# A one-core inference step: first expert rows prepared for two experts at a time, 22 leading weight slots instead of 20, residual rows behind the second expert, gathers of 96 rows

## The chip, the cores and the metric

The kernel runs on one core of a Trainium2 chip. TensorE does the matmuls, VectorE and ScalarE move and scale results, GpSimd issues the gathers, and SyncE issues the weight transfers; 16 DMA engines carry them out. The metric is the device time of one execution in microseconds, as the median of several runs.

## The reference

One layer of a hybrid encoder over 256 prompt tokens and 32 sample tokens, all in fp32. An attention and a recurrent branch are mixed and added to x; then a mixture of experts follows, the part that matters here:

```python
def hmoe(h, wg, bg, ws, bs, wu, wd):
    ...
    _, g_idx = lax.top_k(g_logits, 1)
    ...
    e_val, e_idx = lax.top_k(sub_sel, TOP_K)
    ...
    for e in range(N_EXPERTS):
        gate, up = jnp.split(hf @ wu[e], 2, axis=-1)
        out = out + combine[:, e:e + 1] * ((jax.nn.silu(gate) * up) @ wd[e])
```

There are 16 experts in 4 groups of 4. A token picks one group and two experts in it. An expert has 2048 x 1024 up-weights (8 MB) and 512 x 2048 down-weights (4 MB), so 192 MB of expert weights are read.

## The kernel before

The program is one stream of instructions for each engine, joined by semaphores. Up to about 1187 us it computes the projections, the two branches and W_O, with a ring of four weight tiles. Then a router stage picks groups and experts, and after it the expert stage reads all 16 experts.

**Pieces and slots.** Expert weights come in 192 pieces of 1 MB, in the order of `STREAM`: eight up-pieces of expert 0, then a mix in which two up-pieces of the next expert and one down-piece of this one alternate. Piece n goes to slot `SLOT[n]`. There are 16 permanent slots (`PERM`) and 4 that are used once (`ONCE`), because they lie in memory that later holds something else: two under `yo` and `gain`, two under the second half of `hgs`. SyncE's loop has a wait ahead of some pieces: n = 14 for the end of W_O, n = 17 for the x1 rows to be written out, the first gather and its tail (`x1_out`, `token_ps`, `xs_in`). From n = 20 a piece waits until TensorE has used the piece that was last in its slot (`eh_done`). For n = 20 to 32 that is piece n - 20, from n = 33 on piece n - 16. Down-pieces of the last expert are cut by halves.

**Rows of a group.** For a group of experts (`g`), GpSimd gathers the up to 96 token rows of that group from x1 in memory into `xs` (`rows_in`, L688). `spread` (L1421) multiplies them with one-hot matrices `R`, so that `hgs` holds the rows, transposed, in 64 slots of each of four experts: 16 blocks k of 128 channels. ScalarE and VectorE drain each step with the norm's gain `gup` (`drain_spread`). For group 0 there are four such steps q, with two spreads to each engine: q = 0 and 1 before the first piece, q = 2 and 3 ahead of half-pieces t = 2 and t = 4 (`SPREAD_AT`). For the next groups they lie among the down-pieces of the third expert of the group before.

**Half-pieces.** The expert loop counts t from 0 to 383, two for each piece. `column_pair` (L1396) does the four matmuls of a half. `row_turn` (L1411, L1415) turns the one-hot matrices at t = 8 (`FIRST_ROWS`); `act_turn` (L1453) turns an expert's activation before its down-pieces, which begin at `DOWN_AT` (20, 44, 68, ... for experts 0, 1, 2). `meta_turn` (L1405) makes the next group's metadata at `META_AT`, the next rows are turned at `ROWS_AT`, and `residual` (L1446) adds the gathered rows to the four output banks at `RESIDUAL_AT`, which also frees `xs` for the next gather. In the kernel before all of these stand in the down-phase of a group's first expert. `add_rows` (L1462) adds an expert's result to the output banks. `keep_warm` issues matmuls whose result nobody reads.

Of the kernel before, what the change touches and what calls it, by code (L numbers as in the profile page):

```python
# [14 lines left out]
F32 = mybir.dt.float32  # L15
# [7 lines left out]
P = 128  # L23
# [27 lines left out]
PERM, ONCE = 16, 4  # L51
# [23 lines left out]
SLOT = [*range(13), *range(PERM, LEAD), *range(13, PERM)] + [n % PERM for n in range(PIECES - LEAD)]  # L75
# [43 lines left out]
NCONST, NCONST2 = 21, 13  # L119

# [33 lines left out]
def build(nc, x_prompt, x_sample, cache_k, cache_v, state_conv, state_lru, norm1_g, w_in, conv_w,  # L154
# [128 lines left out]
    lgT = sb("lgT", [40, T])  # L283
    best = sb("best", [TB, 5, 5 * FT, 4])
# [7 lines left out]
    hgs = sb("hgs", [P, 2, KT, EPG, ES])  # L292
    at_hgs1 = here[0] - 2 * 8192
# [33 lines left out]
    xs = sb("xs", [P, D])  # L327
    at_yo = here[0]
    yo = sb("yo", [CAP, D])
    gain = sb("gain", [P, D])  # L330
# [30 lines left out]
    up_v = expert_w_up[0].rearrange("e (p k) n -> p e k n", k=KT)  # L361
# [11 lines left out]
    with ExitStack() as ctx:  # L373
# [10 lines left out]
        trio = [bank[0:2], bank[2:4], bank[4:6]]  # L384

        x_in = [sem(f"x_in{f}") for f in range(FT)]
        par_in, rw_in, gain_in, gup_in = sem("par_in"), sem("rw_in"), sem("gain_in"), sem("gup_in")
# [58 lines left out]
        def spread_bank(q, c):  # L446

            return trio[q % 3][c] if q < SPREAD else work
# [15 lines left out]
        def _(sp):  # L464
# [12 lines left out]
            sp.dma_start(gup[:, :], norm2_g[0].rearrange("(p k) -> p k", k=KT)).then_inc(gup_in, 16)  # L477
# [53 lines left out]
            for dst, src in ((wr[:, :, 0:4], router_group_w[0].rearrange("(k p) g -> p k g", p=P)),  # L531
# [4 lines left out]
                sp.dma_start(dst, src).then_inc(rw_in, 16)  # L536
            gated_loads(T_PA, COL["ga"], w_pa_v)

            def fetch(slot, e, s, by_half=False):

                dst = raw[slot][:, :]
                if s < PU:
                    src = up_v[:, e, 2 * s:2 * s + 2, :]
                    dst = dst.rearrange("p (a k n) -> p a k n", a=1, k=2)
# [19 lines left out]
            for n, (e, s) in enumerate(STREAM):  # L564
# [41 lines left out]
        def _(pool):  # L606
# [122 lines left out]
        def _(a):  # L729
# [247 lines left out]

            def drain_spread(q):

                a.wait_ge(spreadA_ps, q + 1)  # L980
                for c in range(2):
                    k = 4 * (q % SPREAD) + c
                    ins = a.activation(hgs[:, q // SPREAD % 2, k, :, :].rearrange("p e s -> p (e s)"),
                                       spread_bank(q, 0)[:, 256 * c:256 * (c + 1)], ACT.Copy, scale=gup[:, k:k + 1])
# [58 lines left out]
            a.wait_ge(gup_in, 16)  # L1043
            for q in range(2):
                drain_spread(q)
            for t in range(HALF_N):
# [16 lines left out]
                if t == FIRST_ROWS:  # L1063
                    rows(0, bank[2])
# [3 lines left out]
                for q, at in enumerate(SPREAD_AT):  # L1068
                    if t == at[0]:
# [14 lines left out]
            with a.If(n > CAP):  # L1084
                def again(v, first, width):

                    with a.Fori(0, NG) as g:
                        with a.Fori(0, width) as w:
# [5 lines left out]
                            for k in range(KT):  # L1094
                                a.wait_ge(ovhg_ps, KT * it + k + 1)
                                a.activation(hgs[:, 0, k, :, :].rearrange("p e s -> p (e s)"),
                                             bank[4 + k % 4][:, 0:EPG * ES], ACT.Copy, scale=gup[:, k:k + 1])\
# [29 lines left out]
        def _(pe):  # L1127
            pe.wait_ge(consts2, NCONST2)
            pe.wait_ge(par_in, 16 * 9)
# [1005 lines left out]
```

## Time and profile before

| what | value |
|---|---|
| median of 3 runs | 1687.1 us (1686.56 to 1687.59) |
| profiled execution, its time | 1686.14 us |
| profiled execution, its span | 1684.3 us |
| TensorE busy | 1610.3 us, 96% |
| VectorE, ScalarE, GpSimd busy | 720.2, 639.7, 139.1 us |
| DMA, SyncE's queue | 383.31 MB in 391456 packets |

Busy time of TensorE is modelled and holds matmuls that wait in a pipeline, so its 96% alone doesn't say that it bounds the kernel. The time of the profiled execution is 1.8 us more than its span, and 1.0 us less than the median.

### The profile page before, as it was taken

The page shows a single profiled execution, that of the slowest core. Times are in us where ns is not written, and L with a number is a line of the kernel's source. Part 1 is how long each engine was busy: PE and PEld are TensorE (multiplying, and loading weights), DVE is VectorE, ACT ScalarE, POOL GpSimd, SP SyncE. Part 2 cuts the span into 40 slices and gives each one's busy share as a digit, 9 for nine tenths or more (in the row PEclk, how much of TensorE's full clock was granted, in tenths as well). Part 3 has the DMA queues.
Part 4 walks back from the last instruction along what each step waited for, and adds up shares of the span by engine and source line. Part 5 has one row for each costly group of instructions (what it writes and reads, how often), then busy time and mean ns, then how long its engine had stood idle before and what let it go on. Part 6 is the DMA issues. An engine that isn't in the chain of part 4 may idle for free. (4 is left out here: it accounts for less than half of the span.)

```text
span 1684.3 us, 27482 instructions
## 1 busy us (share of the span) xinstructions
PE 1610.3 (96%) x10714; PEld 1295.7 (77%) x10714; DVE 720.2 (43%) x1072; ACT 639.7 (38%) x1078; POOL 139.1 (8%) x189
## 2 busy tenths in 40 slices
PE   5999999999999999999999999999999999989885
PEld 4999999999999999999999999999734334323221
DVE  5888886443445455455454444544310201101101
ACT  6666665333344444444443333544211211111202
POOL 1644441000000000000000000000000000000000
PEclk9999999999999999999999999999999999999998
DMA  8465556566656546546478567795899999999995
GB/s 215 129 165 159 152 160 177 150 172 177 189 145 190 146 139 189 151 133 187 86 202 217 150 168 188 207 298 180 301 359 422 421 421 421 421 421 421 422 421 233
DMA packets 404519, 400.28 MB, mean 238 GB/s; under 512 B 19504, under 2 KB 377248, under 8 KB 379392
## 3 DMA queue, kind: packets, MB, share of 16 engines
q1 hardware_dynamic: 391456, 383.31, 69.2%
q0 software_dynamic: 2560, 11.21, 2.1%
q10 hardware_dynamic: 10432, 4.79, 1.1%
q8 instruction: 47, 0.77, 0.2%
q14 instruction: 24, 0.20, 0.0%
HBM read 389.77 MB, written 13.43 MB: 239 GB/s over the span
## 5 line engine op out<-in xcount | busy, mean ns | idle before, releaser
L1164 PE MATMUL bank<-hH,wH 128*128 128x288 f32 x1792 | 536.1, 299 | 6.2 <-ACTq L799 2.7
L1615 DVE TENSOR_TENSOR wL<-ring,wH 128x1024 fp32r<-128x1024 f32 x320 | 387.9, 1230 | 353.7 <-ACT wH L736 346.1
L736 ACT ACTIVATE wH<-ring 128x1024 fp32r<-128x1024 f32 x320 | 335.6, 1058 | 517.3 <-PE bank L1166 446.8
L1165 PE MATMUL bank<-hL,wH 128*128 128x288 f32 x1792 | 528.9, 295 | 0.0
L1166 PE MATMUL bank<-hH,wL 128*128 128x288 f32 x1792 | 528.5, 295 | 0.0
L1164 PEld LDWEIGHTS bank<-hH,wH 128*128 128x128 f32 x1792 | 337.3, 188 | 13.5 <-issue 7.0
L1165 PEld LDWEIGHTS bank<-hL,wH 128*128 128x128 f32 x1792 | 337.4, 188 | 0.3
L1166 PEld LDWEIGHTS bank<-hH,wL 128*128 128x128 f32 x1792 | 337.2, 188 | 0.0
L1396 PE MATMUL bank<-raw,hgs 128*64 128x512 f32 x1024 | 242.7, 600 | 18.9 <-DMA raw<-in_expert_w_up 15.3
L1396 PEld LDWEIGHTS bank<-raw,hgs 128*64 128x64 f32 x1024 | 66.6, 136 | 162.2 <-issue 110.5
L1164 PE MATMUL bank<-oH,wH 128*128 128x288 f32 x512 | 150.7, 294 | 0.5 <-DVE oL L1712 0.5
L1165 PE MATMUL bank<-oL,wH 128*128 128x288 f32 x512 | 151.0, 295 | 0.0
L1166 PE MATMUL bank<-oH,wL 128*128 128x288 f32 x512 | 150.9, 295 | 0.0
L1396 PE MATMUL bank<-raw,actT 128*64 128x512 f32 x512 | 124.7, 601 | 8.3 <-DMA raw<-in_expert_w_down 7.8
L1984 DVE SCALAR_TENSOR_TENSOR silu<-bank,es,silu 64x512 f32<-64x512 f32 x16 | 12.1, 757 | 265.7 <-ACT silu L1020 265.7
L1164 PEld LDWEIGHTS bank<-oH,wH 128*128 128x128 f32 x512 | 96.3, 188 | 1.0 <-DVE oL L1712 0.7
L1165 PEld LDWEIGHTS bank<-oL,wH 128*128 128x128 f32 x512 | 96.3, 188 | 0.0
L1166 PEld LDWEIGHTS bank<-oH,wL 128*128 128x128 f32 x512 | 96.2, 188 | 0.0
L1396 PEld LDWEIGHTS bank<-raw,actT 128*64 128x64 f32 x512 | 32.9, 136 | 78.3 <-issue 56.8
L1020 ACT ACTIVATE silu<-bank,es 64x512 f32<-64x512 f32 x16 | 10.9, 681 | 198.7 <-PE bank L1396 198.6
L1350 PE MATMUL bank<-hH,wH 128*128 128x288 f32 x256 | 76.4, 299 | 0.0
L1351 PE MATMUL bank<-hL,wH 128*128 128x288 f32 x256 | 75.5, 295 | 0.0
(312 smaller groups left out, 1538.4 us busy)
## 6 DMA issues: line engine op xcount, KB each, us to landing
raw<-in_expert_w_up SPq DMA_DIRECT2D x128, 1024.0 KB, 26.0
ring<-in_w_in SPq DMA_DIRECT2D x112, 1024.0 KB, 6.3
raw<-in_expert_w_down SPq DMA_DIRECT2D x64, 1024.0 KB, 26.5
ring<-in_w_pb SPq DMA_DIRECT2D x16, 1024.0 KB, 9.1
ring<-in_w_pa SPq DMA_DIRECT2D x16, 1024.0 KB, 9.1
ring<-in_w_o SPq DMA_DIRECT2D x16, 1024.0 KB, 6.1
cK<-in_cache_k SPq DMA_DIRECT2D x16, 256.0 KB, 2.8
cV<-in_cache_v SPq DMA_DIRECT2D x16, 256.0 KB, 3.2
```

The costliest lines, as they stand in the source:

```text
L736: a.activation(wH[2 * (slot % 2) + half][:, :, :], ring[slot][:, 8 * half:8 * half + 8, :], ACT.Copy).then_inc(hi_ready, 1)
L1020: a.activation(silu[ES:P, :], upb[0:ES, :], ACT.Silu, scale=es[0:ES, e // EPG % 2, e % EPG, 4:5]).then_inc(silu_ready, 1)
L1164: pe.matmul(dst, hi, rH[:, k, :], start=(k == 0), stop=False)
L1165: pe.matmul(dst, hi, rL[:, k, :], start=False, stop=False)
L1166: ins = pe.matmul(dst, lo, rH[:, k, :], start=False, stop=(k == KT - 1))
L1350: pe.matmul(dst, hi, hH[:, k, :], start=(k == 0), stop=False, skip_group_check=True)
L1351: pe.matmul(dst, hi, hL[:, k, :], start=False, stop=False, skip_group_check=True)
L1396: ins = pe.matmul(dst[c * ES:(c + 1) * ES, :], w, raw[slot][:, 1024 * half + 512 * c:1024 * half + 512 * (c + 1)], start=first, stop=last)
L1615: v.tensor_tensor(lo[:, :, :], ring[slot][:, 8 * half:8 * half + 8, :], hi[:, :, :].bitcast(F32), ALU.subtract).then_inc(lo_ready, 1)
L1984: v.scalar_tensor_tensor(silu[ES:P, :], upb[ES:P, :], es[ES:P, e // EPG % 2, e % EPG, e % EPG:e % EPG + 1], silu[ES:P, :], ALU.mult, ALU.m ...
```

## The change

- **Slots.** Six single-use slots instead of four, 22 leading pieces instead of 20. They lie under `yo` and `gain` (two), under the part of `hgs` for experts 2 and 3 of group 0 (one), under the second half of `hgs` (two), and under the scratch of W_O's end, where `yH` and `yL` will be (one). `hgs` is laid out by pairs of experts. SyncE's wait for the end of W_O moves from n = 14 to n = 13, the wait for x1 and the gather from n = 17 to n = 18. The first piece that waits for n - 16 is now n = 35.
- **First rows by pairs.** For group 0 a spread makes 128 columns, for two experts. The first pair has two steps of eight spreads: q = 0 before the first piece, q = 1 at t = 4 and t = 8. The second pair follows at t = 31, 33, 35 and 37. `FIRST_ROWS` moves from t = 8 to t = 12 and to another bank.
- **Channel order.** Block k now holds channels of the two-by-two order `(s p k)`: `spread` reads `xs` with a step of 2 elements instead of 16, up-pieces are one run of 1 MB in memory, and `gup` is read as 1024 runs of 8 bytes instead of 128 of 64, on the semaphore that TensorE's first instruction waits for.
- **Next group's work and residual** move from the down-phase of a group's first expert to that of its second; `add_rows` of the first expert now starts the sum, and the residual is added to it.
- **96 rows** in the gathers and in `gain`, not 128. A memset of unused indices is gone. `keep_warm(14)` instead of `keep_warm(6)` ahead of the metadata.

```diff
-PERM, ONCE = 16, 4
+PERM, ONCE = 16, 6
...
-SLOT = [*range(13), *range(PERM, LEAD), *range(13, PERM)] + [n % PERM for n in range(PIECES - LEAD)]
+SLOT = [*range(13), PERM + 2, PERM, PERM + 1, *range(PERM + 3, LEAD), *range(13, PERM)] + [n % PERM for n in range(PIECES - LEAD)]
...
-ASSIGN_AT = [DOWN_AT[EPG * g] for g in range(NG - 1)]
-META_AT = [DOWN_AT[EPG * g] + 2 for g in range(NG - 1)]
-ROWS_AT = [DOWN_AT[EPG * g] + 6 for g in range(NG - 1)]
-RESIDUAL_AT = [DOWN_AT[EPG * g] + 10 for g in range(NG)]
-FIRST_ROWS = 8
-SPREAD_AT = [(None, None)] * 2 + [(2, 2), (4, 4)]
+ASSIGN_AT = [DOWN_AT[EPG * g + 1] for g in range(NG - 1)]
+META_AT = [DOWN_AT[EPG * g + 1] + 2 for g in range(NG - 1)]
+ROWS_AT = [DOWN_AT[EPG * g + 1] + 6 for g in range(NG - 1)]
+RESIDUAL_AT = [DOWN_AT[EPG * g + 1] + 4 for g in range(NG)]
+FIRST_ROWS = 12
+SPREAD_AT = [(None, None), (4, 8)] + [(DOWN_AT[0] + 11 + 4 * r, DOWN_AT[0] + 13 + 4 * r) for r in range(2)]
...
-    hgs = sb("hgs", [P, 2, KT, EPG, ES])
-    at_hgs1 = here[0] - 2 * 8192
+    at_hgs = here[0]
+    hgs = sb("hgs", [P, 2, 2, KT, 2, ES])
...
-    xs = sb("xs", [P, D])
+    xs = sb("xs", [CAP, D])
...
-    here[0] = at_hgs1
-    raw += [sb(f"raw{s}", [P, 2048]) for s in range(PERM + 2, LEAD)]
+    here[0] = at_hgs + 8192
+    raw += [sb(f"raw{s}", [P, 2048]) for s in range(PERM + 2, PERM + 5)]
     assert here[0] <= at_o
+    here[0] = at_prow
+    raw += [sb(f"raw{s}", [P, 2048]) for s in range(PERM + 5, LEAD)]
...
-    up_v = expert_w_up[0].rearrange("e (p k) n -> p e k n", k=KT)
+    up_v = expert_w_up[0].rearrange("e (s p k) n -> p e s k n", p=P, k=2)
...
-            return trio[q % 3][c] if q < SPREAD else work
+            return out4[2 * q + c] if q < 2 else work
...
-            sp.dma_start(gup[:, :], norm2_g[0].rearrange("(p k) -> p k", k=KT)).then_inc(gup_in, 16)
+            sp.dma_start(gup[:, :].rearrange("p (s k) -> p s k", k=2),
+                         norm2_g[0].rearrange("(s p k) -> p s k", p=P, k=2)).then_inc(par_in, 16)
...
-                elif n == 14:
+                elif n == 13:
                     sp.wait_ge(half_done, 2 * T_END)
-                elif n == 17:
+                elif n == 18:
+                    sp.wait_ge(lg_ps, 1)
                     sp.wait_ge(x1_out, 16 * len(X1_PARTS) + 16)
                     sp.wait_ge(token_ps, 2)
                     sp.wait_ge(xs_in, 16)
...
-                    sp.dma_start(gain[:, :], final_norm_g.rearrange("(a n) -> a n", a=1).partition_broadcast(P))\
+                    sp.dma_start(gain[:, :], final_norm_g.rearrange("(a n) -> a n", a=1).partition_broadcast(CAP))\
...
-                                            bass.IndirectOffsetOnAxis(ap=idx[:, column, 2:3], axis=0),
+                                            bass.IndirectOffsetOnAxis(ap=idx[0:CAP, column, 2:3], axis=0),
...
-                    pool.wait_ge(outB, SPREAD * (g + 1))
...
+            def drain_pair(q):
+
+                a.wait_ge(spreadA_ps, q + 1)
+                for c in range(4):
+                    k = 8 * (q % 2) + 4 + c
+                    ins = a.activation(hgs[:, 0, q // 2, k, :, :].rearrange("p e s -> p (e s)"),
+                                       spread_bank(q, 1)[:, P * c:P * (c + 1)], ACT.Copy, scale=gup[:, k:k + 1])
+                ins.then_inc(outA, 1)
...
-            a.wait_ge(gup_in, 16)
-            for q in range(2):
-                drain_spread(q)
+            a.wait_ge(par_in, 16 * NPARAM)
+            drain_pair(0)
...
-            def spread(dst, k):
-
-                return pe.matmul(dst.rearrange("p (e s) -> p e s", e=EPG), xs[0:CAP, k::KT], R[:, :, 0, :].bitcast(F32),
+            def spread(dst, k, first=0, count=EPG):
+
+                c = 2 * P * (k // 2) + k % 2
+                return pe.matmul(dst.rearrange("p (e s) -> p e s", e=count), xs[:, c:c + 2 * P - 1:2],
+                                 R[:, first:first + count, 0, :].bitcast(F32),
                                  start=True, stop=True, skip_group_check=True)
 
+            def pair_step(q, c):
+
+                if q >= 2 and c == 0:
+                    need(pe, outA, q if q > 2 else 0)
+                elif q >= 2:
+                    pe.wait_ge(outB, q + 1)
+                if q == 0 and c == 0:
+                    pe.wait_ge(xs_in, 16)
+                    pe.wait_ge(R_ready, 1)
+                if q == 1 and c == 1:
+                    pe.wait_ge(last_ready, 1)
+                dst = spread_bank(q, c)
+                for kk in range(4):
+                    ins = spread(dst[:, P * kk:P * (kk + 1)], 8 * (q % 2) + 4 * c + kk, 2 * (q // 2), 2)
+                ins.then_inc((spreadB_ps, spreadA_ps)[c], 1)
...
-            keep_warm(6)
+            keep_warm(14)
             pe.wait_ge(meta_ready, 1)
             meta_turn(0, bank[6])
             keep_warm(20)
-            for q in range(2):
-                spread_step(q, 0)
-                spread_step(q, 1)
+            pair_step(0, 0)
+            pair_step(0, 1)
...
-                    if j == 0 and g > 0:
+                    if j == 0 and g > 0 or e == 2:
                         pe.wait_ge(outA, SPREAD * (g + 1))
...
                 if e == 0 and s < PU and half == 0:
-                    pe.wait_ge((outA, outB)[s % 2], s // 2 + 1)
+                    pe.wait_ge((outB, outA)[s // 2 % 2], s // 4 + 1)
...
-                    add_rows((e - 1) // EPG % 2, (e - 1) % EPG, j == 0)
+                    if j == 1:
+                        pe.wait_ge(es_ready, g + 1)
+                        pe.wait_ge(RT_ready, g + 1)
+                        need(pe, scaled_ready, 4 * g)
+                    add_rows((e - 1) // EPG % 2, (e - 1) % EPG, j == 0, j == 1)
...
                 for g_ in range(NG):
                     if t == RESIDUAL_AT[g_]:
-                        pe.wait_ge(es_ready, g_ + 1)
-                        pe.wait_ge(RT_ready, g_ + 1)
-                        need(pe, scaled_ready, 4 * g_)
-                        residual().then_inc(xs_free, 1)
+                        residual(False).then_inc(xs_free, 1)
...
-            own.step(v.memset(idx[CAP:P, :, 2:3], 0))
...
+            def drain_pair(q):
+
+                v.wait_ge(spreadB_ps, q + 1)
+                k = 8 * (q % 2)
+                v.tensor_tensor(hgs[:, 0, q // 2, k:k + 4, :, :].rearrange("p k e s -> p k (e s)"),
+                                spread_bank(q, 0)[:, :].rearrange("p (k c) -> p k c", k=4),
+                                gup[:, k:k + 4].rearrange("p (k a) -> p k a", a=1).to_broadcast([P, 4, 2 * ES]),
+                                ALU.mult).then_inc(outB, 1)
```

TensorE at the start of the expert stage, before the change. R and xs are the spreads, raw the weight pieces by buffer number, ms and ident the row turn:

```order
L1320 MATMUL bank<-hH 128x288 x20
L1421 MATMUL bank<-R,xs 128x256 x8
L1396 MATMUL bank<-raw_136,hgs 64x512 x4
L1421 MATMUL bank<-R,xs 128x256 x4
L1396 MATMUL bank<-raw_137,hgs 64x512 x4
L1421 MATMUL bank<-R,xs 128x256 x4
L1396 MATMUL bank<-raw_138,hgs 64x512 x4
L1396 MATMUL bank<-raw_139,hgs 64x512 x4
L1411 MATMUL bank<-ident,R 128x96 x4
L1415 MATMUL bank<-ms,R 128x5 x4
```

The same place after it:

```order
L1336 MATMUL bank<-hH 128x288 x20
L1438 MATMUL bank<-R,xs 128x128 x8
L1412 MATMUL bank<-raw_136,hgs 64x512 x4
L1412 MATMUL bank<-raw_137,hgs 64x512 x4
L1438 MATMUL bank<-R,xs 128x128 x4
L1412 MATMUL bank<-raw_138,hgs 64x512 x4
L1412 MATMUL bank<-raw_139,hgs 64x512 x4
L1438 MATMUL bank<-R,xs 128x128 x4
L1412 MATMUL bank<-raw_140,hgs 64x512 x4
L1412 MATMUL bank<-raw_141,hgs 64x512 x4
L1427 MATMUL bank<-ident,R 128x96 x4
L1431 MATMUL bank<-ms,R 128x5 x4
```

There are as many spreads ahead of the row turn, 16, each of half the columns, and they stand further apart.

TensorE in the down-phase of expert 0, before the change, from its first down-piece (raw_181) to the last piece that stands ahead of the limit (the one behind raw_190):

```order
L1396 MATMUL bank<-raw_181,actT 64x512 x4
L1405 MATMUL bank<-meta,G 96x12 x3
L1396 MATMUL bank<-raw_182,hgs 64x512 x4
L1396 MATMUL bank<-raw_183,hgs 64x512 x4
L1411 MATMUL bank<-ident,R 128x96 x4
L1415 MATMUL bank<-ms,R 128x5 x4
L1396 MATMUL bank<-raw_187,actT 64x512 x4
L1396 MATMUL bank<-raw_188,hgs 64x512 x4
L1446 MATMUL bank<-xs,ident 96x512 x4
L1396 MATMUL bank<-raw_189,hgs 64x512 x4
L1396 MATMUL bank<-raw_190,actT 64x512 x4
L1396 MATMUL bank<-raw_160,hgs 64x512 x4
```

The same down-phase after it, from the sixth piece on, with the rows around the second pair:

```order
L1412 MATMUL bank<-raw_188,hgs 64x512 x2
L1438 MATMUL bank<-R,xs 128x128 x4
L1412 MATMUL bank<-raw_188,hgs 64x512 x2
L1412 MATMUL bank<-raw_190,actT 64x512 x2
L1438 MATMUL bank<-R,xs 128x128 x4
L1412 MATMUL bank<-raw_190,actT 64x512 x2
L1412 MATMUL bank<-raw_191,hgs 64x512 x2
L1438 MATMUL bank<-R,xs 128x128 x4
L1412 MATMUL bank<-raw_191,hgs 64x512 x2
L1412 MATMUL bank<-raw_192,hgs 64x512 x2
L1438 MATMUL bank<-R,xs 128x128 x4
L1412 MATMUL bank<-raw_192,hgs 64x512 x2
```

The metadata turn, the row turn and the residual have left this phase, and four steps of four spreads have come into it.

## Rows read from the trace of the kernel before

**Rows 1.** Page, the span in 40 slices: DMA busy, in tenths.
```profile
DMA  8465556566656546546478567795899999999995
```

**Rows 2.** Waits, 1600 to 1665 us: total, times, longest.
```profile
PE bank L1396 <- DMA raw<-in_expert_w_up: 6.1, 11, 0.6
```

**Rows 3.** Stretches: length, busy of each engine (instructions), granted clock, DMA share, GB/s.
```profile
1200.00:1205.00 5.00, 5.00 (x27) 5.00 (x27) 1.52 (x9) 0.00 (x0) 0.00 (x0) 0.66 0.59 209
1225.00:1230.00 5.00, 3.37 (x18) 1.01 (x16) 1.02 (x3) 0.68 (x1) 0.00 (x0) 1.00 1.00 390
1245.00:1250.00 5.00, 5.00 (x16) 1.61 (x16) 0.00 (x0) 0.00 (x0) 0.74 (x1) 1.00 0.64 262
1250.00:1255.00 5.00, 5.00 (x26) 1.72 (x24) 0.00 (x0) 0.00 (x0) 1.35 (x2) 1.00 0.74 228
1300.00:1340.00 40.00, 40.00 (x186) 14.49 (x184) 5.66 (x8) 5.79 (x12) 0.00 (x0) 1.00 1.01 421
```

**Rows 4.** Timeline of SyncE: start us, us, then line, operation and count.
```profile
1180.52 0.43 SPq L552 DMA_DIRECT2D raw<-in_expert_w_down  x1
1187.76 1.07 SPq L552 DMA_DIRECT2D raw<-in_expert_w_up  x2
1188.88 0.66 SPq L552 DMA_DIRECT2D raw<-in_expert_w_down  x1
...
1239.91 14.12 SPq L552 DMA_DIRECT2D raw<-in_expert_w_up  x2
```

**Rows 5.** Timeline of TensorE, matmul records: start, us, operation, count, [idle before].
```profile
1199.73 0.68 PE L1405 MATMUL bank<-meta,G 96*96 96x12 f32 x6 [1.32 <-DVEq L1948]
1200.26 4.43 PE L1320 MATMUL bank<-hH 128*128 128x288 f32 x20
1204.53 3.81 PE L1421 MATMUL bank<-R,xs 96*128 96x256 f32 x16
1208.27 1.94 PE L1396 MATMUL bank<-raw,hgs 128*64 128x512 f32 x8
1210.14 2.15 PE L1421 MATMUL bank<-R,xs 96*128 96x256 f32 x8
...
1219.74 0.55 PE L1411 MATMUL bank<-ident,R 96*128 96x96 f32 x4
...
1221.04 7.09 PE L1396 MATMUL bank<-raw,hgs 128*64 128x512 f32 x32
1229.76 1.94 PE L1396 MATMUL bank<-raw,hgs 128*64 128x512 f32 x8 [1.63 <-DVE silu L1984]
...
1235.60 0.68 PE L1405 MATMUL bank<-meta,G 96*96 96x12 f32 x6
...
1244.68 3.67 PE L1446 MATMUL bank<-xs,ident 96*96 96x512 f32 x8
```

**Rows 6.** Timeline of GpSimd, 1190 to 1255 us.
```profile
1198.02 1.12 POOL L688 DMA_INDIRECT xs<-x_rows,idx  x1 [10.32 <-DVE idx L1925]
```

**Rows 7.** DMA issues, us to landing: 1187 to 1200, then 1265 to 1600.
```profile
xs<-x_rows,idx POOLq DMA_INDIRECT x1, 6.1
...
xs<-x_rows,idx POOLq DMA_INDIRECT x2, 9.8
```

**Rows 8.** Groups, 1190 to 1260 us: busy us, mean ns, idle before.
```profile
L1421 PEld LDWEIGHTS bank<-R,xs 96*128 96x128 f32 x32 | 7.3, 307 | 1.6 <-issue 1.6
...
L1975 DVE TENSOR_TENSOR hgs<-bank,gup 128x512 f32<-128x512 f32 x4 | 2.8, 691 | 12.1 <-PE bank L1421 12.1
...
L1415 PEld LDWEIGHTS bank<-ms,R 96*128 96x128 f32 x16 | 1.9, 192 | 0.0
```

**Rows 9.** DMA packets, 16 to 20 us, then 838 to 840 us.
```profile
DMA packets 2365, 1.20 MB, mean 301 GB/s; under 512 B 16, under 2 KB 2365, under 8 KB 2365
...
DMA packets 3625, 0.06 MB, mean 29 GB/s; under 512 B 3625, under 2 KB 3625, under 8 KB 3625
```

**Rows 10.** Timeline of ScalarE, 0 to 30 us.
```profile
19.16 2.00 ACT L736 ACTIVATE wH<-ring 128x1024 fp32r<-128x1024 f32 x2 [1.90 <-DMA ring<-in_w_in]
```

More of the change, by code:

```diff
@@ L283, in build @@
     lgT = sb("lgT", [40, T])
+    here[0] = max(here[0], at_prow + 8192)
     best = sb("best", [TB, 5, 5 * FT, 4])
@@ L982, in drain_spread @@
                     k = 4 * (q % SPREAD) + c
-                    ins = a.activation(hgs[:, q // SPREAD % 2, k, :, :].rearrange("p e s -> p (e s)"),
-                                       spread_bank(q, 0)[:, 256 * c:256 * (c + 1)], ACT.Copy, scale=gup[:, k:k + 1])
+                    ins = a.activation(hgs[:, q // SPREAD % 2, :, k, :, :].rearrange("p a e s -> p a (e s)"),
+                                       work[:, 256 * c:256 * (c + 1)].rearrange("p (a c) -> p a c", a=2),
+                                       ACT.Copy, scale=gup[:, k:k + 1])
                 ins.then_inc(outA, 1)
@@ L1063, in _ @@
                 if t == FIRST_ROWS:
-                    rows(0, bank[2])
+                    rows(0, bank[4])
                 for g in range(NG - 1):
@@ L1068, in _ @@
                 for q, at in enumerate(SPREAD_AT):
-                    if t == at[0]:
+                    if q < SPREAD and t == at[1]:
+                        drain_pair(q)
+                    elif q >= SPREAD and t == at[0]:
                         drain_spread(q)
@@ L1432, in spread_step @@
                     pe.wait_ge(outA, q + 1)
-                if q == 0 and c == 0:
-                    pe.wait_ge(last_ready, 1)
                 if r == 0 and c == 0:
@@ L1437, in spread_step, with residual @@
                     pe.wait_ge(R_ready, n + 1)
-                dst = spread_bank(q, c)
                 for kk in range(2):
-                    ins = spread(dst[:, 256 * kk:256 * (kk + 1)], 4 * r + 2 * c + kk)
+                    ins = spread(work[:, 256 * kk:256 * (kk + 1)], 4 * r + 2 * c + kk)
                 ins.then_inc((spreadA_ps, spreadB_ps)[c], 1)
-            def residual():
+            def residual(first):
                 for nb in range(4):
-                    ins = pe.matmul(out4[nb][0:CAP, :], ident[0:CAP, 0:CAP], xs[0:CAP, nb * 512:(nb + 1) * 512],
-                                    start=True, stop=False, skip_group_check=True)
+                    ins = pe.matmul(out4[nb][0:CAP, :], ident[0:CAP, 0:CAP], xs[:, nb * 512:(nb + 1) * 512],
+                                    start=first, stop=False, skip_group_check=True)
                 return ins
@@ L1454, in act_turn, with add_rows @@
                 ins.then_inc(at_ps, 1)
-            def add_rows(buf, j, last):
+            def add_rows(buf, j, last, first=False):
                 for half in range(2):
@@ L1462, in add_rows @@
                             ins = pe.matmul(out4[2 * half + c][0:CAP, :], RT[rows, buf, j, :], y[rows, half, :],
-                                            start=False, stop=last and y is yL, skip_group_check=True)
+                                            start=first and y is yH, stop=last and y is yL, skip_group_check=True)
                     ins.then_inc(sum_ps, 1)
@@ L1495, in _ @@
                     if t == TURN_AT[x]:
-                        if x % EPG == 1 and x // EPG + 1 < NG:
+                        if x % EPG == 2 and x // EPG + 1 < NG:
                             pe.wait_ge(RT_ready, x // EPG + 2)
@@ L1565, in again @@
                         pe.wait_ge(xs_in, 32 * (NG + nth) + 16)
-                        residual()
+                        residual(True)
                         with pe.Fori(0, width) as w:
@@ L2023, in _ @@
             v.tensor_copy(cnt_i[:, :], cmax[:, :]).then_inc(routed, 1)
-            v.wait_ge(gup_in, 16)
-            for q in range(2):
-                drain_spread(q)
+            v.wait_ge(par_in, 16 * NPARAM)
+            drain_pair(0)
             for t in range(HALF_N):
@@ L2041, in _ @@
                 if t == FIRST_ROWS:
-                    columns(bank[2], 0, 0)
+                    columns(bank[4], 0, 0)
                 for g in range(NG - 1):
@@ L2052, in _ @@
                 for q, at in enumerate(SPREAD_AT):
-                    if t == at[1]:
+                    if q < SPREAD and t == at[0]:
+                        drain_pair(q)
+                    elif q >= SPREAD and t == at[1]:
                         drain_spread(q)
```

49 lines of the change are left out of this document (27 added, 22 removed).

## The prediction

> **What bounds the kernel now.** I read the page's forty slices first [rows 1]: the DMA engines are busy 4 to 8 tenths in the first 26 slices, and 9 tenths or more in every slice from 30 to 39. The last third, the expert stage, is held by the weight stream. Its pieces are 1 MB each (1.049 million bytes), and at the steady 421 GB/s one takes 2.49 us. That TensorE has no part in it at the end is shown by its own waits [rows 2]: between 1600 and 1665 us it waits 11 times for up-weights that have not landed.
>
> A stream that never pauses ends when it was last allowed to pause plus its remaining bytes. So the question is where it last pauses. The stretches [rows 3] answer: 421 GB/s at 1300, but 262 and 228 GB/s in the ten microseconds from 1245. SyncE's issues [rows 4] say why. The 14.12 us row covers pieces 32 and 33, and its second issue comes at its end, near 1253.7. Piece 33 is the first whose slot (13) was last filled by piece 17 instead of piece 13: the four single-use slots drop out there, so the stream may be only 16 ahead of TensorE instead of 20. By 1245 all pieces up to 32 are in, and SyncE waits until TensorE has used piece 17. **The end is therefore set by TensorE's start of the expert stage, up to piece 17, and by how many pieces are in by then**, and not by the 430 us behind it.
>
> TensorE's timeline [rows 5] prices that start. The rows for the first slots are filled by 16 spreads of 256 columns: eight take 3.81 us, and four between two pieces 2.15 us. The first up-matmul starts at 1208.27. Four pieces take 7.09 us, 1.78 a piece. The first row turn takes 1.30 us (1219.74 to 1221.04), the wait for the first activation 1.63 us, the metadata turn 0.68 and the residual rows 3.67 us. The gather of the first rows was issued at 1198.02 [rows 6] and took 6.1 us [rows 7], so it landed at 1204.1; the first spread is at 1204.53.
>
> **The change, part by part.**
>
> *Slots.* 22 leading slots instead of 20. The limit moves: the first piece that may be only 16 ahead is now 35, and it waits for piece 19. I therefore need the new time at which piece 19 is used. Everything behind it is 157 pieces instead of 159, worth 2 x 2.49 = 5.0 us.
>
> *When piece 19 is used.* Start: the gather lands at 1204.3 (below). Eight spreads of 128 columns and the drain of the first four: 2.15 us. This spread is not in the trace. The nearest full-width loads with few columns behind them are in the row turn: 12 matmul records in 1.30 us, 0.11 each. A spread is two records, so four spreads are 8 x 0.12 = 0.96, and 1.1 with the change-over between pieces; that is the value I take. The low bound is 0.9 us for four; the upper is 2.15, the price of today's 256 columns, or even 2.46 (8 x 0.307) if each weight load showed in full. The first pair needs 1.0 us to its first drain, then 0.69 us of VectorE [rows 8] and some 0.4 of semaphores, which makes 2.15. Then 20 pieces at 1.78 = 35.6; six more steps of four spreads (two for the first pair, four for the second) = 6.6; row turn 1.3, activation wait 1.63, the turn of silu 0.4 (four records of at most the row turn's size). Sum: 1204.3 + 2.15 + 35.6 + 6.6 + 3.33 = 1252.0, against 1253.7. **Minus 1.7 us.** The metadata turn, second row turn and residual no longer stand ahead of the limit; they cost the same later, behind piece 22. There pieces 20 to 26 take TensorE 12.5 us, with the turn 0.4, the metadata 0.7, the residual 3.7, the rows 1.3 and the sum over the first expert's rows (by half the residual, 1.8) 20.4 us. In that time the queue has 7 x 2.49 of pieces, a gather of 1.9 and the gain load of 1.9, 21.2 us of transfers. So I cost the move at nothing. Without the gather and the gain as cover it would cost 20.4 - 17.4 = 3.0 us.
>
> Why the spread should reach the low price: the weight load with elements 16 apart takes 307 ns, the one of the same size with adjacent elements 192 ns [rows 8]. The new layout reads elements 2 apart. Today's pass costs 3.81/16 = 0.238 us, 0.05 more than a 192 ns load. The Trainium skill (SBUF — State Buffer, Door 1: The DMA port swizzle) says that SBUF is read in 16-byte lines and that two hits in a line keep full bandwidth: a step of two fp32 values gives two hits, a step of 16 one. The 307 against 192 agrees with it; no run here shows the step of two. By that rule the sum stands as made; without it, by the third rival.
>
> *Does the stream reach piece 34 first?* Before the gather, five pieces are issued together at the end of W_O where three are now [rows 4]: piece 13 moved back from 1180.52 to about 1187.8, and one new. They run to about 1202.8 (three ended near 1197.8, plus 2 x 2.49). The next four go when the tail of x1 is out, about 1205.5, and start moving near 1207. 17 pieces (18 to 34) then end at 1249.4, ahead of 1252.0. The remaining pause is some 3 us. It also caps what a still faster TensorE could win at 4 us more.
>
> *The gather.* It shares the engines with those five pieces until 1202.8, and has 96 rows, not 128 (1.75 instead of 2.3 us of bytes at 421 GB/s). Alone it takes 6.1, under the full stream 9.8 [rows 7]. The overlap is about half of its flight but the bytes are fewer, so I take 6.3 and land at 1204.3; the bounds are 5.5 and 9.8.
>
> *Gathers and gain behind the limit.* Gain is 96 rows: minus 0.6 us. Before, two gathers of 1.05 MB (2.5 us) lay behind the restart, and one in the pause; now three of 0.79 MB (1.87): plus 0.6 us.
>
> *Warm matmuls.* Before, TensorE idled 1.32 us ahead of the metadata turn, and the granted clock was 0.66 in the stretch from 1200 [rows 3, 5], that is mostly at 1.2 GHz, so 20 warm matmuls took 4.43 us. With 14 instead of 6 the idle time goes; the 20 then end near 1203.2, ahead of the gather. Gain: about 0.2 us, in the start above.
>
> *The start of the kernel.* gup is now 1024 pieces of 8 bytes instead of 128 of 64, ahead of the first weights in SyncE's queue, and ScalarE's first split waits for those weights [rows 10]. The router loads (16-byte pieces) moved 3625 packets in 2 us on 16 engines, 8.8 ns each [rows 9]. 56 more on each engine: plus 0.5 us, with nothing to hide it, since TensorE is busy from there to 1187. Bounds 0 and 1.5 (56 times 27 ns, the pace of the 512-byte packets of w_in in the first 20 us: 2365 in 4 us on 16 engines). The Trainium skill (DMA: Bandwidth & Descriptors, Specifications) warns that below 512 B the engine reads, modifies and writes. It speaks against this part; by the router loads' packets, which are below that size too, it costs the 0.5 of the sum; by a slow read-modify-write the upper bound or more.
>
> *At nothing:* the memset that goes (0.1 us, counted), the up-weights read as one run of 1 MB (down pieces already are, and the stretch that holds both kinds stands at 9 tenths or more in every slice [rows 1]), other drains, the later start of the sum.
>
> **Sum:** -1.7 - 5.0 - 0.6 + 0.6 + 0.5 - 0.1 = -6.3 us. The profiled execution took 1686.14 us (span 1684.3), 1.0 below the median 1687.1; it gives 1679.8, and from the median 1680.8, which I predict.
>
> **The rivals.**
> 1. *The gather pays the full stream.* It lands after 9.8 us, at 1207.8: 3.5 us later, all of it on piece 19. Time 1684.3. For it: the extra pieces lie in just this stretch. Against: they end at 1202.8.
> 2. *The clock falls while TensorE waits for the gather.* An idle of 1.32 us came before a stretch at 1.2 GHz (0.66 over 5 us is 3.4 us at half speed); but 1.63 us at 1228 did not, the clock stayed 1.00 [rows 3, 5]. Price 1.7 us: 1682.5.
> 3. *Spreads keep today's price* (2.07 for four, 3.8 for eight): the start grows by 1.65 and six steps by 5.8; piece 19 at 1259.5, 5.8 after 1253.7 instead of 1.7 before it, so 7.5 more than the sum: 1688.3. No change.
> 4. *The spreads cost more than now per byte of work,* 2.46 us for four because each load of 0.307 shows: the start grows by 3.05 and six steps by 8.15; piece 19 at 1263.2. Time 1692.0, slower. It decides at 1.9 us for four, where the sum is zero (6.3 over eight steps is 0.8 on 1.1). Against: today's passes take 0.238, less than their load.
> 5. *The start costs 1.5:* 1681.8.
> 6. *The two slots change nothing,* because their bytes are hidden anyway: excluded by the pause at 1245 and the later waits [rows 2, 3].
>
> **From this the numbers.** Main case 0.61 (own range 1678.5 to 1683.0), rival 1 0.12, rival 2 0.08, rival 5 0.05, rival 3 0.07, rival 4 0.07. 0.2% is 3.4 us, about what a measurement of this kernel can tell from no change. Rival 1 is 2.8 us below the median, so it counts as no change in half of its spread. Faster 0.79, same 0.14, slower 0.07. The range 1677.5 to 1687.0 leaves out rivals 3 and 4 and a little below, where the cap of 4 us would be used up.
>
> **What would show it.** Right: the 14 us pause of SyncE is gone or short, piece 35 leaves near 1252 (plus 0.5 for the start); four spreads of 128 columns take about 1 us; their weight load is near 192 ns; the gather lands within 7 us; 421 GB/s from 1255 on; the first matmul is 0.5 us later. Wrong: a second pause between 1255 and 1275; spreads over 1.9 us; TensorE at 0.5 clock near 1206; a gather of 9 us; the first matmul 1.5 us late or more.

## The result and the profile after

The changed kernel took 1700.05 us (median of 4 executions, 1698.65 to 1701.07) against 1686.83 (1686.49 to 1687.59) for the kernel before on the same chip: a ratio of 1.0077, with a 95% interval of 1.006 to 1.0095. I had forecast 6.3 us less; it is 13 us more. An interval that excludes 1 shows a difference; none of the differences here reaches 2%. Its profiled execution took 1698.65 us with a span of 1696.9 (before: 1684.3).

The page of the kernel after, the span in 40 slices:

```profile
DMA  9466556565756546645577666784889999999995
GB/s 212 129 165 162 153 161 169 153 179 162 195 146 178 167 135 169 179 130 158 122 193 190 180 163 181 228 289 163 346 323 376 422 400 422 421 401 421 422 421 222
```

The DMA row looks like the one of before [rows 1]: 9 tenths at the end. The row under it does not. Slices 33 and 36 show 400 and 401 GB/s at a full busy share, where their neighbours have 421 or 422. Busy engines moved less; whoever reads only the busy digits misses it.

SyncE's timeline after, the part that answers to [rows 4]:

```profile
1181.02 0.33 SPq L556 DMA_DIRECT2D raw<-in_expert_w_up  x1
1188.62 0.33 SPq L556 DMA_DIRECT2D raw<-in_expert_w_down  x1
1188.99 1.40 SPq L556 DMA_DIRECT2D raw<-in_expert_w_up  x2
1190.43 0.76 SPq L556 DMA_DIRECT2D raw<-in_expert_w_down  x1
1191.23 18.66 SPq L556 DMA_DIRECT2D raw<-in_expert_w_up  x2
...
1243.48 0.33 SPq L556 DMA_DIRECT2D raw<-in_expert_w_down  x1
1260.66 2.27 SPq L556 DMA_DIRECT2D raw<-in_expert_w_up  x2
```

Five pieces leave between 1188.6 and 1191.3; the second of the row of 18.66 us is piece 18, which waits for the gather. The pause in SyncE's issues, which I wanted short, is longer than before: 17 us, until piece 35 leaves at 1260.66 (forecast: 1252.0).

GpSimd's and TensorE's timelines and the DMA issues after, for [rows 5 to 7]:

```profile
1198.80 1.07 POOL L693 DMA_INDIRECT xs<-x_rows,idx  x1 [10.23 <-DVE idx L1958]
```

```profile
xs<-x_rows,idx POOLq DMA_INDIRECT x1, 10.3
```

```profile
1200.45 0.68 PE L1421 MATMUL bank<-meta,G 96*96 96x12 f32 x6 [0.22 <-DVEq L1981]
1200.98 2.91 PE L1336 MATMUL bank<-hH 128*128 128x288 f32 x20
1209.14 3.78 PE L1438 MATMUL bank<-R,xs 96*128 96x128 f32 x16 [5.25 <-DMA xs<-x_rows,idx]
1212.86 5.28 PE L1412 MATMUL bank<-raw,hgs 128*64 128x512 f32 x16
1218.07 1.21 PE L1438 MATMUL bank<-R,xs 96*128 96x128 f32 x8
```

The warm matmuls do what I said (20 in 2.91 us, after 0.22 us of idle time). Then TensorE stands still for 5.25 us, because the gather takes 10.3 us and not 6.1. Behind that idle time eight spreads take 3.78 us and four pieces 5.28; the four spreads at 1218.07 take 1.21 (1.13 from start to start).

Stretches of the kernel after (columns as in [rows 3]):

```profile
1205.00:1210.00 5.00, 0.86 (x4) 0.86 (x5) 0.00 (x0) 0.00 (x0) 0.00 (x0) 0.59 0.41 109
1210.00:1215.00 5.00, 5.00 (x20) 3.40 (x21) 0.69 (x1) 1.14 (x4) 0.00 (x0) 0.50 0.84 324
...
1273.00:1278.00 5.00, 5.00 (x29) 2.25 (x29) 0.18 (x1) 0.49 (x1) 2.00 (x2) 1.00 1.05 262
1280.00:1286.00 6.00, 6.00 (x30) 2.02 (x28) 0.00 (x0) 0.00 (x0) 0.00 (x0) 1.00 1.01 273
1300.00:1340.00 40.00, 40.00 (x182) 14.51 (x180) 4.40 (x7) 4.78 (x10) 0.00 (x0) 1.00 1.01 421
1387.00:1392.00 5.00, 5.00 (x26) 1.63 (x24) 0.00 (x0) 0.00 (x0) 0.00 (x0) 1.00 1.00 274
```

Two things are new. The granted clock is 0.50 (1.2 GHz) after TensorE's idle time. And while the gain load (1273 to 1278) and the gathers (1280, 1387) run, the engines are fully busy at 262 to 274 GB/s instead of 421.

The span splits into two numbers that the experiments can be read by: when piece 35 (before: piece 33) leaves, and what lies behind it. Before: 1253.7 and 430.6 us. After: 1260.7 and 436.2. Forecast: 1252.0 and 425.6. The second number is what is left of the span, so the two always add up to it.

### The profile page after: what moved, and what is told of

Its sections match the earlier page's. It is cut to its first block and busy times, and to the rows that moved or that the text cites. A ratio compares the mean times of both kernels' runs of the same rounds, so it can differ in the third digit from the quotient of the medians.

```text
span 1696.9 us, 27574 instructions
## 1 busy us (share of the span) xinstructions
PE 1615.4 (95%) x10754; PEld 1292.5 (76%) x10754; DVE 720.2 (42%) x1071; ACT 641.0 (38%) x1086; POOL 138.9 (8%) x189
## 5 line engine op out<-in xcount | busy, mean ns | idle before, releaser
L1182 PE MATMUL bank<-hH,wL 128*128 128x288 f32 x1792 | 528.7, 295 | 0.0
L1412 PE MATMUL bank<-raw,hgs 128*64 128x512 f32 x1024 | 246.8, 608 | 23.6 <-DMA raw<-in_expert_w_up 20.1
L1368 PE MATMUL bank<-hH,wL 128*128 128x288 f32 x256 | 75.3, 294 | 0.0
```

Source lines behind the costliest of these rows:

```text
L1182: ins = pe.matmul(dst, lo, rH[:, k, :], start=False, stop=(k == KT - 1))
L1368: ins = pe.matmul(dst, lo, hH[:, k, :], start=False, stop=False, skip_group_check=True)
L1412: ins = pe.matmul(dst[c * ES:(c + 1) * ES, :], w, raw[slot][:, 1024 * half + 512 * c:1024 * half + 512 * (c + 1)], start=first, stop=last)
```

## Experiments

Theory: a transfer of 96 rows slows all DMA engines, and the first gather is late. Rival: the rows mean nothing, and the gather is late because five pieces are ahead of it where three were. All ratios are to the kernel before, timed beside each; its medians there were 1687.65 to 1688.9.

**1 to 4: the rows.** In the changed kernel and in the one before, gathers and gain apart:

```
-    xs = sb("xs", [CAP, D])
+    xs = sb("xs", [P, D])
-  ... IndirectOffsetOnAxis(ap=idx[0:CAP, column, 2:3], axis=0)
+  ... IndirectOffsetOnAxis(ap=idx[:, column, 2:3], axis=0)
+            own.step(v.memset(idx[CAP:P, :, 2:3], 0))
```

The changed kernel with gathers of 128 rows:


> The changed kernel with its gathers of 128 rows again (the index memset with it; the gain load stays at 96 rows). Theory A, a transfer of 96 rows slows all 16 DMA engines while it runs: each of the two gathers behind the limit stops costing 3 to 4 us (421 GB/s through 1380 to 1390 instead of 277), and the first gather lands in 6 to 8 us instead of 10.3, so that TensorE idles under 3 us before the first spread and the clock stays up; piece 35 leaves near 1254, end 1683 to 1689. Rival B, the gather is late because five pieces share the engines with it, and the number of rows means nothing: landing stays 10 us, the clock falls to 0.5 as before, piece 35 leaves at 1260, and the time stays within 2 us of 1700.

And with the gain load of 128 rows too (`partition_broadcast(P)`):


> As the run before, and the gain load broadcast to 128 rows again. Theory A: another 2 to 4 us faster than with the gain at 96 rows, since the stretch from 1272 to 1285 with 271 to 284 GB/s goes; 1680 to 1686. Rival B: no change, or 0.6 us slower by the larger load.

The kernel before with gathers of 96 rows, then with only the gain load of 96:


> The kernel before with only its gathers cut to 96 rows. Theory A: two gathers behind the limit at 3 to 4 us each, and the first gather lands 1 to 4 us later: 1692 to 1698 against 1686.8. Rival B: 1.2 us fewer bytes, 1685.5 to 1687.

> The kernel before with only the gain load cut to 96 rows. Theory A: plus 2 to 4 us, if the load runs behind the limit, none if it falls into the pause at 1245. Rival B: minus 0.6 us.

Measured, in this order: 1693.3 us, ratio 1.0028 (1.0018 to 1.0038); 1692.15, 1.0021 (1.0012 to 1.003); 1691.09, 1.0018 (1.0009 to 1.0027); 1690.22, 1.0009 (1.0 to 1.0018). By the ratios, 128 rows for both give back 9.5 us against the timing above (1.0077) and 5.4 us against the second timing of the same kernel (run 13, 1.0053). Gathers of 96 rows alone cost the kernel before 3 us. For its gain load alone the interval reaches 1.0, and only the trace shows a cost: behind the pause the two variants need 433.9 and 433.6 us against 430.6. Stretches of the second run, to compare with the ones above:

```profile
1273.00:1278.00 5.00, 5.00 (x29) 2.25 (x29) 0.18 (x1) 0.49 (x1) 2.09 (x2) 1.00 1.02 428
1280.00:1286.00 6.00, 6.00 (x30) 2.02 (x28) 0.00 (x0) 0.00 (x0) 0.00 (x0) 1.00 1.02 421
1387.00:1392.00 5.00, 5.00 (x26) 1.63 (x24) 0.00 (x0) 0.00 (x0) 0.00 (x0) 1.00 1.01 413
```

More bytes, and no slow stretch. In the first run, where only the gain load still has 96 rows, only its stretch is slow:

```profile
1273.00:1278.00 5.00, 5.00 (x28) 2.26 (x28) 0.18 (x1) 0.28 (x1) 2.09 (x2) 1.00 1.02 275
```

But the half of my theory on the first gather fell: it still lands after 9.7 and 9.6 us, piece 35 still leaves at 1261.1 and 1260.8, and the clock is still 0.50 after 1210. There the rival is right: the rows don't make it late. All of the gain lies behind the pause: 431.1 and 430.8 us against 436.2.

**5 and 8: the pieces ahead of the gather.** With 128 rows, the wait for the gather moves forward; in the second, piece 13 also gets its old slot and leaves at 1181 again.

```
-                elif n == 18:
+                elif n == 16:        (17 in the second)
                     ...
                     sp.wait_ge(xs_in, 16)
```

> The changed kernel with gathers and gain of 128 rows, and in addition pieces 16 and 17 wait for the gather's landing (the wait that stands at piece 18 moves to 16), so that three pieces share the engines with it as in the kernel before, not five. Theory (contention makes the first gather late, and TensorE's idle time then drops its clock): landing within 7 us instead of 9.7, TensorE idle under 2 us before the first spread, granted clock 0.9 or more from 1205 to 1215, piece 35 leaves 5 to 8 us earlier than in the run with 128 rows (1253 to 1256 against 1260.8), and the time is 1684 to 1687 against 1692.2. Pieces 16 and 17 come 5 us later, which the pause after 1254 takes up. Rival (the gather is late for another reason, its place in the program or its queue): landing stays near 10 us, time 1692 or more.

> As the first of these runs, but with piece 13 in the slot that it had in the kernel before, so that it leaves at 1181 instead of 1189 and fills the time from 1186 to 1189 in which the DMA engines now stand still; the wait for the gather stands at piece 17. Three pieces again share the engines with the gather. The first gather lands within 7 us, piece 35 leaves at 1253 to 1256; one more piece is in by then, which counts only if the stream is what comes late (17 to 19 pieces of 2.49 us from 1206 end at 1250 to 1254, TensorE's use of piece 19 falls at 1253). So 0 to 2.5 us less than the first of these runs: 1683 to 1686.

Measured: 1685.15 us, 0.9981 (0.9972 to 0.999); and 1685.35, 0.9982 (0.9973 to 0.9991). Both as expected, and both faster than the kernel before. TensorE's timeline of the first:

```profile
1201.82 2.91 PE L1336 MATMUL bank<-hH 128*128 128x288 f32 x20
1205.83 2.15 PE L1438 MATMUL bank<-R,xs 96*128 96x128 f32 x16 [1.10 <-DMA xs<-x_rows,idx]
1207.95 3.65 PE L1412 MATMUL bank<-raw,hgs 128*64 128x512 f32 x16
```

The gather was issued at 1199.58 and took 6.2 us; eight spreads take 2.15 us and four pieces 3.65; piece 35 leaves at 1254.13. The piece gained in the second run adds nothing: it leaves at 1254.02, so TensorE sets that moment.

How the gather queues shows in stretches of the kernel after and then of the first of these runs:

```profile
1198.00:1203.00 5.00, 4.78 (x39) 4.55 (x38) 3.59 (x24) 1.28 (x3) 1.80 (x2) 1.00 1.01 421
1203.00:1207.00 4.00, 0.89 (x7) 0.66 (x5) 0.00 (x0) 0.00 (x0) 0.00 (x0) 0.87 0.99 263
1207.00:1209.00 2.00, 0.00 (x0) 0.00 (x0) 0.00 (x0) 0.00 (x0) 0.00 (x0) 0.50 0.12 43
```

```profile
1198.00:1203.00 5.00, 4.75 (x41) 4.52 (x41) 3.56 (x24) 1.85 (x4) 1.86 (x2) 1.00 0.62 188
1203.00:1207.00 4.00, 2.90 (x24) 2.67 (x22) 0.56 (x4) 0.00 (x0) 0.00 (x0) 1.00 0.47 187
```

After, the engines run at 421 GB/s until 1203, the rate of the weight stream, and then 4 us at 263. The queues of the kernel after say whose bytes these are (packets, MB, share), first from 1198 to 1203, then from 1203 to 1207; q1 is SyncE's queue, q0 GpSimd's:

```profile
q1 hardware_dynamic: 287, 2.09, 99.6%
...
q0 software_dynamic: 145, 0.82, 76.4%
q1 hardware_dynamic: 43, 0.23, 22.2%
```

In the 4.2 us after its issue the gather moves no packet. The five pieces are nearly through by 1203, about when I said, and its rows mostly follow them instead of running beside them.

**6: the clock.** With 128 rows and no hold, 50 instead of 20 warm matmuls (`keep_warm(50)`), so that TensorE works while the gather is late.

> The changed kernel with 128 rows and 50 instead of 20 warm matmuls before the first spread (4.4 us more of them, as long as the idle time was). The gather lands as late as before. Theory (the clock fell because TensorE was idle 4.6 us): granted clock 1.00 throughout, the eight spreads take 2.2 us instead of 3.8 and the first four pieces' matmuls 1.9 instead of 3.1 to 3.6 each two; 3.5 to 4 us faster than with 20, 1688 to 1689. Rival (the clock fell for the stage's own power, whatever the idle): clock 0.5 after 1209 again, 1692 to 1693.

Measured: 1688.69 us, 1.0001 (0.9992 to 1.001), against 1.0021 without them: 3.4 us.

```profile
1202.37 6.91 PE L1336 MATMUL bank<-hH 128*128 128x288 f32 x50
1209.98 2.15 PE L1438 MATMUL bank<-R,xs 96*128 96x128 f32 x16 [0.70 <-DMA xs<-x_rows,idx]
```

The gather is as late as without them (issued at 1200.13, first spread at 1209.98), but the granted clock stays at 1.00 in every stretch from 1200 to 1215. So idle time took the clock, and the late gather costs twice: 3.4 us by itself (this run against the one with the hold) and 3.4 us by the clock behind it.

**7: the moved residual.** `RESIDUAL_AT` eight half-pieces later, with 128 rows.

> The changed kernel with 128 rows, and the residual rows (3.7 us of TensorE) four pieces later, behind pieces that the stream no longer waits for. Theory (the move of the next group's work behind the second expert is not free: each piece behind the limit waits for TensorE to use one 16 before, and the 3.7 us stand just there): the first 10 us behind the pause move 330 to 345 GB/s instead of 303, time 1 to 2 us less than with the residual where the change put it, 1690.5 to 1691. Rival (the move costs nothing): within 0.5 us of 1692.2.

Measured: 1691.8 us, 1.0022 (1.0013 to 1.0031) against 1.0021. No gain in the median; the first 10 us behind the pause still move 304 GB/s, not 330 to 345. Its trace needs 430.0 us behind the pause, inside the scatter of the runs with 128 rows (below). What stands in those 10 us is the turn, the sum over the first expert's rows and the metadata turn, not the residual. The theory of this run fell.

**9: the layout.** The run with the hold at 16, with the channel order, the up-weights' layout and the gup load of the kernel before. The wait for the last channels' rows (`last_ready`) moves ahead of the first spread with it, since every spread now reads some of them. The edit changes all of these at once; the rows below say which of them counts.

```
-                c = 2 * P * (k // 2) + k % 2
-                ... xs[0:CAP, c:c + 2 * P - 1:2]
+                ... xs[0:CAP, k::KT]
```

> The best version so far (128 rows, pieces 16 and 17 held until the gather has landed) with the channel order of the kernel before: a slot's rows hold channels 16 apart, so the spread's weight load reads elements 16 apart again, and gup comes in 128 pieces of 64 bytes. If the load's step of 2 is what makes four spreads of 128 columns take 1.2 us: they now take 2.1 to 2.5 us (load 307 ns), eight such steps stand ahead of piece 19, it is used 7 to 10 us later, and the time is 1692 to 1695. The front of the kernel tells the price of the 8-byte pieces of gup: W_O's first load leaves 0.5 to 1 us earlier than the 1038.8 us of the run that this one changes, if they cost anything. If the step means nothing: 1684 to 1686.

Measured: 1693.03 us, 1.003 (1.0019 to 1.004), 8 us more. Its groups of weight loads, and two of TensorE's rows:

```profile
L1436 PEld LDWEIGHTS bank<-R,xs 96*128 96x128 f32 x160 | 37.5, 307 | 25.7 <-issue 23.5 <-DMA xs<-x_rows,idx 1.4 <-ACT hgs L986 0.8
```

```profile
1205.82 3.86 PE L1436 MATMUL bank<-R,xs 96*128 96x128 f32 x16 [1.15 <-DMA xs<-x_rows,idx]
...
1213.98 2.01 PE L1436 MATMUL bank<-R,xs 96*128 96x128 f32 x8
```

With a step of 16 the load takes 307 ns, with a step of 2 it takes 195 (the group of the run with the hold). Half as many columns then save next to nothing: eight spreads take 3.86 us, as long as the eight of 256 columns before [rows 5], and four take 2.01 against 2.15. Piece 35 leaves 7.2 us later, at 1261.38. W_O's first load leaves at 1038.77 against 1038.82, and the first split of the weights waits until 18.65 us against 18.80, so the 8-byte pieces of gup cost 0.15 us at most in these two traces.

**10: the warm matmuls alone.** The kernel before with `keep_warm(14)` instead of 6.

> The kernel before with 14 instead of 6 warm matmuls ahead of the metadata turn, nothing else. If the idle time of 1.3 us there is what lets the clock fall in some executions (granted 0.66 and 0.55 after 1200 in two profiles of it, 1.00 in a third): the idle time is 0.2 us, the 20 warm matmuls take 2.9 us in each, the spread between executions shrinks, and the median is 1 to 2 us below that of the kernel before. If the clock falls for another reason: no change, and some executions still show it.

Measured: 1687.14 us (1686.34 to 1689.2), 0.9997 (0.9988 to 1.0007). The median does not move. The clock of its 11 executions lies between 0.994 and 0.997, that of the 27 of the kernel before between 0.991 and 0.996, so the worst ones are gone; that is all this run can say.

**11 and 12: do the losses add, and is it 96?** First the changed kernel with 96 rows and only the hold; then the version with the hold and 128 rows, with gathers of 112.

> The changed kernel with its 96 rows, and only the wait for the gather moved from piece 18 to 16. If the late gather and the slow 96-row transfers are two separate losses that add up: piece 35 leaves at 1253 to 1255, the stretches of 270 to 290 GB/s for each gather and the gain load stay, and the time is 7 to 8 us above the same kernel with 128 rows (1685.2), 1692 to 1694. If one loss hides in the other: 1700 or 1686.

> The best version so far with gathers of 112 rows instead of 128. By bytes alone it is 0.3 us less a gather, 1684.4. If 96 rows cost only because part of the destinations is hit by 8 rows and part by 4 (the Trainium skill, SBUF — State Buffer, Door 1: The DMA port swizzle, has ports 0 to 14 serve the first 64 partitions and the odd ones the rest): 112 rows still take as long as 128, no change, 1685. If it is any number of rows other than 128 that slows the engines, since each engine's share of the rows then no longer goes where its share of the weight stream goes: the stretches at the two gathers behind the pause again show under 350 GB/s at a full DMA share, and the time is 1687 to 1690.

Measured: 1692.55 us, 1.0026 (1.0015 to 1.0036); and 1691.77, 1.002 (1.0011 to 1.0029). The losses add: piece 35 leaves at 1254.84, and the rest takes 436.3 us. And 112 rows cost nearly as much as 96, though they miss 128 by an eighth. Stretches of the run with 112, then of the one with 128:

```profile
1272.00:1279.00 7.00, 7.00 (x34) 2.31 (x32) 0.00 (x0) 0.00 (x0) 0.00 (x0) 1.00 1.03 274
1380.00:1386.00 6.00, 6.00 (x32) 2.00 (x28) 0.00 (x0) 0.00 (x0) 0.00 (x0) 1.00 1.01 270
```

```profile
1272.00:1279.00 7.00, 7.00 (x34) 2.31 (x32) 0.00 (x0) 0.00 (x0) 0.00 (x0) 1.00 1.00 415
1380.00:1386.00 6.00, 6.00 (x32) 2.01 (x28) 0.00 (x0) 0.00 (x0) 0.00 (x0) 1.00 1.02 414
```

At 1380, 6 us times (414 - 270) GB/s is 0.86 MB, or 2.1 us of stream for one gather; three are 6.2 us, and the run is 6.6 slower. What the expectation took from the unbalanced ports alone (no change) is refuted.

**13 and 14: the changed kernel again, and the combination** (128 rows, piece 13 at 1181, hold at 17, 26 warm matmuls, residual later), on one chip.

> The changed kernel as it is, on the chip of the next run. If the parts account for it (7.4 us for the 96 rows, 6.9 us for the late gather with the clock, on top of 1685.2 us): 1699 to 1700. If something else is in it: more than 1 us off.

> 128 rows, piece 13 in its old slot and leaving at 1181, the wait for the gather at piece 17, 26 warm matmuls before the first spread, the residual rows four pieces later. Each was worth 0 to 0.4 us by itself beyond the hold, so 1684 to 1685.5 with the kernel before at 1687.7 to 1688.4; ratio 0.998.

Measured: 1697.66 us, 1.0053 (1.0039 to 1.0067), 1.3 us under what I expected, more than the 1 us that I had allowed; and 1685.53, 0.9982 (0.9973 to 0.9992). The combination is no better than the hold alone.

## Why the prediction was wrong

**Right in part:** the bound. The time hangs on when TensorE has used piece 19: with the hold piece 35 leaves 6.6 us earlier than without it and the median falls by 7.0, with the old layout it leaves 7.2 us later and the median rises by 7.9. But I took the 430 us behind it as given but for bytes, and 5.6 us of the loss lie there. The price of four spreads was right (1.1 us; 1.13 measured), as was the reason for it, the step of the load (195 ns against 307). I had the rule on 16-byte lines from the Trainium skill (SBUF — State Buffer, Door 1: The DMA port swizzle); the run with the old layout agrees with it. From the gather's issue to piece 35 my sum had 53.98 us, and the undisturbed run has 54.55. That run (1254.13 and 431.0 us) is 3.3 us faster than the kernel before, about half of the forecast. No run changes the number of slots alone, so what the two slots are worth by themselves is not shown.

**The step "The gather".** "The overlap is about half of its flight but the bytes are fewer, so I take 6.3." It took 10.3. That was rival 1's mechanism, with a chance of 0.12. My argument against it ("they end at 1202.8") was true and no argument: the gather's rows come behind the pieces, so it lands some 6 us after they end. "It shares the engines with those five pieces" is the overlap that failed: until 1203 it shared nothing. Cost on piece 35: 4.0 us.

**Rival 2** was priced alone at 1.7 us. I let it stand for an idle time of 1.3 us and did not ask what rival 1 would do to it. With 5.25 us of idle time the eight spreads cost 1.63 us more and the first four pieces 1.63 (3.78 - 2.15, 5.28 - 3.65), 3.3 in all. Two rivals of one cause are one case, at 1688, not two at 1684 and 1682.5.

Piece 35 is thus 8.7 us later than forecast: 4.0 gather, 3.3 clock, 0.6 in the sum, and 0.8 because the gather was issued later (1198.80 against 1198.02). That last part is not the change: variants of the kernel before issued it at 1198.7, 1198.9 and 1199.4.

**The step "Gathers and gain behind the limit"** is the larger error. I costed rows by bytes: minus 0.6 for the gain, 0.6 less for each gather. The version with 128 rows needs 430.8 us behind the pause, and the one with 96 needs 436.2. Over all runs of the changed kernel the two sets lie apart: 430.0 to 431.4 us in the eight with gathers of 128 rows, 436.2 to 437.5 in the four with 96 or 112. By bytes it should have been 2.5 us less, not 5.4 more: 7.9 us. The trace before had no such transfer into a tile of under 128 rows in a full stream, and I gave the term no bounds at all. The Trainium skill states the rule that would have warned me (SBUF — State Buffer, The DMA setup-cost knee: for DMA-bound transfers use 128 partitions). Its map of ports (Door 1) has the first 64 partitions on half of them and the rest on the other half; by that 96 rows would take as long as 128, not longer. The trace shows more than that, also at 112 rows, so the map alone does not explain it. My guess in run 12, that each engine's share of the rows no longer goes where its share of the weight stream goes, isn't shown either, and it can't be all: the packets are slow without the stream too. From 1202 to 1205 the first gather has the engines to itself; its queue moves, with 128 rows (run 5) and then with 96 (run 11):

```profile
q0 software_dynamic: 161, 0.94, 86.1%
...
q0 software_dynamic: 112, 0.67, 80.3%
```

That is 0.26 us of an engine's time for a packet against 0.34 (16 engines times 3 us times the share, over the packets). In the stretch from 1280 to 1286 the same working gives 0.20 and 0.35 us for the gather's packets, and for those of the weight stream beside them 0.29 and 0.45. So the slow stretches are shown, and that the weights' packets slow down with the gather's; why they do stays open.

**"So I cost the move at nothing."** Behind the pause the runs with 128 rows need 430.8 us where bytes give 428.1 (425.6 and four times 0.6). The first 10 us behind it move 303 GB/s against 345 in the kernel before, worth 1.0 us. The residual is not what fills them. The other 1.7 us stay open; the scatter from run to run is nearly as large (430.0 to 431.4).

**"The start of the kernel."** 0.5 us forecast, nothing seen: the first split of the weights waits until 18.92 us, before until 19.16 [rows 10].

**Rival 4's price** has a slip: eight spreads of two loads of 0.307 us are 4.9 us, so the start would grow by 2.8 us, not 3.05. Nothing hangs on it.

The parts add up from the other side too: 0.9981 with both repairs, plus 0.0045 for the 96 rows (1.0026 - 0.9981) and 0.004 for the late gather with the clock (1.0021 - 0.9981), makes 1.0066, between the two measured ratios of the changed kernel (1.0053 and 1.0077). The intervals of these two only just overlap; what sets them apart is open.

## What to carry to other kernels

Price a small transfer in a saturated stream by the rate at which the engines run while it is in flight, not by its bytes: trimming three gathers and a load from 128 to 96 rows should have saved 2.5 us by bytes, and behind the pause it cost 5.4. Before more prefetch is issued, look for the one short transfer that TensorE will wait for, and hold the prefetch behind it; here two pieces less in front of the gather were worth 6.8 us, half of that through the clock. Where one rival's outcome is the other's cause, price them together.

## What was unexpected in the hardware

- Gathers of 96 and of 112 rows, and a broadcast load to 96 rows beside the weight stream, each hold the 16 DMA engines at a full busy share and 262 to 275 GB/s for 5 to 7 us; the same with 128 rows leave 413 to 428 GB/s.
- In the changed kernel an idle time of 5.25 us on TensorE was followed by a granted clock of 0.50 in 1210 to 1215. Of about 1.3 us, three executions of the kernel before or of its variants show 0.66, 0.55 and 1.00 in 1200 to 1205; of 1.48 us (run 11) the clock stayed 1.00 in 1205 to 1210.
- Halving the columns of a spread at a step of 16 saved no time (3.81 and 3.86 us for eight); only with a step of 2, where the load takes 195 ns and not 307, did they fall to 2.15.
- A gather issued behind five 1 MB transfers moved no packet for 4.2 us while their queue held the engines at 99.6%.
